# Four sums over the partitions: from products of ones on TensorE to GpSimd

## The chip, the cores and the metric

One core of a Trainium2 chip runs the whole program. The metric is the device time of one execution in microseconds (us); the number quoted for a kernel is the median of several runs. The engines are named as in the profile: PE (TensorE, matmuls), PEld (its weight loads), DVE (VectorE), ACT (ScalarE), POOL (GpSimd) and SP (SyncE, which issues most DMAs).

## The reference

Three transformer layers over 256 tokens of 1024 features, all in fp32: an attention layer with a squared-ReLU feed-forward of 4096 (the "first feed-forward"), then a layer with convolutions and a gated recurrence, then one with stick-breaking attention. The last two ("layer 0" and "layer 1" of the second block) are modulated by a vector `c`:

```
def ada_modulation(c, ada_w, ada_b):
    m = jax.nn.silu(c) @ ada_w + ada_b
    return jnp.split(m, N_MOD, axis=-1)
def modulate(h, shift, scale):
    return h * (1.0 + scale[:, None, :]) + shift[:, None, :]
```

`m` has 6 x 1024 columns: shift, scale and gate for the mixer, and the same for the feed-forward. Layer 0's `m` doesn't depend on the tokens, so it can be computed at any time before layer 0's first norm. Its first 2048 columns are the mixer's shift and scale (`SH_M`, `G_M`).

## The kernel before

**How `m` is made.** The 1024 rows of `ada_w` lie as 8 blocks of 128 partitions. DVE multiplies each block by the column of silu(c) that belongs to it and adds it to a tile `mod` of 128 x 6144 (`ada`, L1330, and `ada_mix`, L1342). What is left is the sum over the 128 partitions, which every partition needs. There are two ways to it in the kernel. `ada_sums` (L2226) is a product on PE with a 128x128 matrix of ones, 512 columns (CH) at a time into a PSUM bank (`sum_bank`), and `ada_parts` (L801) is ACT's copy of the bank back into `mod`. `partition_sums` (L656) is POOL's `partition_all_reduce` in SBUF, also by 512 columns. Sums 0 to 3 (`SH_M`, `G_M`) and 4 to 7 (the mixer's gate and the feed-forward's shift) go by PE, the others of layer 0 and all of layer 1 by POOL.

**Where sums 0 to 3 are.** The first 2048 columns of `mod` are complete when `mix_used` is 16, at the end of the first attention. PE computes sums 0 and 1 just ahead of the norm in front of the first feed-forward, sum 2 behind the transposes of token tile 0 and sum 3 ahead of those of tile 1, inside `entry(U_MLP, ...)`. `entry` is the norm with the first up unit in it: DVE writes the scaled xn, PE transposes it (L1882), ACT rounds it to `aT_hi` (L794), DVE takes the rest `aT_lo`, and PE multiplies (L1924).

**Weights in two parts.** Each weight part (128x1024, half a unit) is loaded to `w_raw` by SP, rounded by ACT to `w_hi` (`split_part`, L735), and DVE subtracts for the rest `w_lo` (`split_part`, L1158); PE multiplies with both. There are four slots. SP loads part v only behind `lo_done` of part v - 4; ACT rounds it only behind `w_used` of part v - 4, which PE counts up at each part that it is done with.

**The first feed-forward** runs 8 slices of 512 hidden features. From slice 1 on, slice j takes two up units into the banks ub and tp (L1910, L1912) and two down units of slice j - 1's hidden features (L1788 to L1791), eight parts in all. In each slice from 2 on DVE makes, in this order: an ada product (128x2048), w_lo of two parts, an addition from PSUM (`mlp_sum`, L1485), an ada product, w_lo of two parts, an addition from PSUM, w_lo of two parts, an ada product, w_lo of two parts, and the rest of the hidden features. The first four of these parts are the down units that PE takes in the same slice, the last four the up units of the next. ACT's relu (L934) waits for the second addition, and only behind relu and square does ACT round the next part. U_MLP is 16, so that `parts_to(U_MLP + 8)` is 48: `w_used` reaches it when PE is done with the up units of slice 2, and the up units of slices 3, 4 and 5 end at 56, 64 and 72.

**POOL** does small work for the norms (`half_var`), sits idle through the first feed-forward, and sums at 336 to 360 us and, four in a row each time, from 411, 484 and 594 us.

Of the kernel before, what the change touches and what calls it, by code (L numbers as in the profile page):

```python
# [39 lines left out]
UNIT = 2048  # L40
# [22 lines left out]
U_MLP = U_WO1 + 4  # L63
U_WIN = U_MLP + 4 * NJ_MLP
# [50 lines left out]
def block_program(nc, a, out):  # L115
    ctx = ExitStack()
    with ctx:
# [125 lines left out]

        def sum_bank(m):

            return (tp[:, 1, :] if m < 4 else acc[:, 1, :], ub[:, 0, :], ub[:, 1, :], acc[:, 2, :])[m % 4]

        def flat(h):
            return h.rearrange("p b n -> p (b n)")
# [363 lines left out]
        def _(pool):  # L613
# [72 lines left out]
            half_var(1, 0)  # L686
            half_var(0, 0)
            half_var(1, 0)
            half_var(0, 0)
            half_var(0, 0)  # L690
            half_var(1, 1)
# [21 lines left out]
        def _(act):  # L713
# [83 lines left out]
            def ada_parts(n0, n1):  # L797

                for n in range(n0, n1):
                    act.wait_ge(ada_sum, n + 1)  # L800
                    act.activation(mod[:, n * CH:(n + 1) * CH], sum_bank(n), ACT.Copy).then_inc(ada_out, 1)  # L801

            def copy_chunk(u, bank, ct):
# [77 lines left out]
            def mlp_norm(u):  # L881

                n_norm[0] += 1
                act.wait_ge(tile0_first, 1)
                half_square(0, 0, acc[:, 0, :], sq_half)
                act.wait_ge(tile0_done, 1)
                half_square(0, 1, acc[:, 1, :], sq_done)
                half_rstd(0, 1, 1)
                act.wait_ge(w_used, parts_to(u - 1))
                half_square(1, 0, acc[:, 2, :], sq_half)  # L890
                act.wait_ge(x_half, 1)
                half_square(0, 0, x[:, 0, 0:CH], sq_half)
                act.wait_ge(x_ready, 1)
                half_square(0, 1, x[:, 0, CH:D], sq_done)
                half_rstd(0, 1, 3)
                act.wait_ge(post_scaled, 2)
                half_square(1, 1, acc[:, 3, :], sq_done)
                half_rstd(1, 1, 2)
                norm_hi(1, 0)
                split_part(2 * u + 2)  # L900
                split_part(2 * u + 3)
                act.wait_ge(x_half, 2)
                half_square(1, 0, x[:, 1, 0:CH], sq_half)
                act.wait_ge(x_ready, 2)
                half_square(1, 1, x[:, 1, CH:D], sq_done)
                half_rstd(1, 1, 4)
                ada_parts(0, 2)
                norm_hi(1, 1)

            mlp_norm(U_MLP)  # L910

            def mlp_first(u):

                ada_parts(2, 4)
                split_hi(u + 2)
                act.wait_ge(w_used, parts_to(u + 2))
                act.activation(gtok, tp[:, :, :], ACT.Relu).then_inc(act_h, 1)
                split_hi(u + 3)
                act.wait_ge(h_T, 1)
                act.activation(hT_hi[:, :, :].rearrange("p (a b) n -> p a b n", a=2), blocks_in(acc[:, 0:2, :]),  # L920
                               ACT.Copy).then_inc(hT_hi_done, 1)
# [220 lines left out]
        def _(dve):  # L1142
# [386 lines left out]
            for j in range(NJ_MLP - 2, NJ_MLP):  # L1529
                mlp_slice(U_MLP + 4 * j - 2, j)  # L1530
            split_part(2 * U_WIN)
            ada_gain(0, 1, ada_out, 4)
            split_part(2 * U_WIN + 1)
            dve.wait_ge(gain_loaded[3], 16)
            dve.wait_ge(ada_gain_done, 1)
# [20 lines left out]
            for step, n in LRU_STEPS:  # L1556
                if step == "L":
                    split_lo(U_WIN + n)
                elif step == "E" and n == 0:
                    copy_chunk(U_WIN, acc[:, 1, :], T0["win"])  # L1560
                elif step == "T":
                    copy_T(uT, T0["win"], 4 * WIN_CHUNKS[n])
                elif step == "M" and n == 6:
                    ada(0, 5, 0, n, 22, dst=mod_next)
                elif step == "M":
                    ada(2, 4, 0, n, 23, src=ada_last, dst=mod_next)
                elif step == "I":
                    ada_gain(0, 4, pool_sum, 2)
                elif step == "P":
                    dve.wait_ge(lru_u, 2)  # L1570
                    dve.tensor_tensor(uT[:, 4:8, :], uT[:, 4:8, :], uT[:, 8:12, :], ALU.mult).then_inc(lru_p, 1)
                elif step == "D" and n == 0:
                    dve.wait_ge(lru_i, 1)
                    dve.wait_ge(lru_xr, 1)
                    dve.tensor_tensor(gate_i, gate_i, xr, ALU.mult).then_inc(lru_ix, 1)
                elif step == "C":
                    dve.wait_ge(cT_a, C0["win"] + 1)
                    dve.wait_ge(cT_v, C0["win"] + 1)
                    conv_last(xr, uT[:, 16:20, :], R_CONV_B, 4, R_CONV_BIAS)
                    conv_taps(xr, uT[:, 16:20, :], R_CONV_B, 4).then_inc(lru_xr, 1)  # L1580
                elif step == "K":
                    dve.wait_ge(lru_tap, 1)
                    conv_taps(conv_a, uT[:, 4:8, :], R_CONV_A, 3).then_inc(lru_conv, 1)
                elif step == "D" and n == 1:
                    dve.wait_ge(lru_a2, 1)
                    dve.wait_ge(lru_t, 1)
                    dve.scalar_tensor_tensor(lru_b, gate_r, 1.0, lru_b, ALU.add, ALU.mult).then_inc(lru_s2, 1)
                elif step == "Q":
                    dve.wait_ge(lru_sqrt, 1)
                    dve.wait_ge(lru_ix, 1)  # L1590
                    chained(dve.tensor_tensor(lru_b, lru_b, gate_i, ALU.mult))
                    for b in range(LB):
                        ins = dve.tensor_tensor_scan(lru_h[:, b, :], lru_a[:, b, :], lru_b[:, b, :], 0.0, ALU.mult, ALU.add)
                    chained(ins)
                elif step == "Y":
                    dve.wait_ge(lru_gelu, 1)
                    dve.tensor_tensor(lru_h, lru_h, uT[:, 12:16, :], ALU.mult).then_inc(lru_yb, 1)
                elif step == "R":
                    dve.wait_ge(lru_yb, 1)
                    dve.wait_ge(y_hi, 1)  # L1600
                    dve.tensor_tensor(hT_lo[:, :, :], lru_h, hT_hi[:, :, :].bitcast(F32),
                                      ALU.subtract).then_inc(y_lo, 1)
                elif step == "Z" and n == 0:
                    dve.wait_ge(lru_u, 3)
                    dve.wait_ge(lru_conv, 1)
                    dve.tensor_tensor(conv_a, conv_a, uT[:, 0:4, :], ALU.mult).then_inc(lru_ya, 1)
                elif step == "Z":
                    dve.wait_ge(y_hi, 2)
                    dve.tensor_tensor(aT_lo[:, 0:LB, :], conv_a, aT_hi[:, 0:LB, :].bitcast(F32),
                                      ALU.subtract).then_inc(y_lo, 1)  # L1610
# [3 lines left out]
            def swiglu(layer):  # L1614
# [49 lines left out]
                        for q in range(2):  # L1664
                            one(u + 5 + 3 * q + 12 * third, 2 + q + 4 * third, i, third if layer == 0 else None)
                if layer == 0:
                    ada_gain(1, 1, pool_sum, 8)
                one(u + 3 * NJ_SG - 4, NJ_SG - 1)

            swiglu(0)  # L1670
# [40 lines left out]
            for step, n in STICK_STEPS:  # L1711
                if step == "L":
                    split_part(2 * U_QKV2 + n)
                elif step == "R":
                    dve.wait_ge(qk_sq_done, n + 1)
                    dve.reduce_sum(qk_ss[:, :], qk_sq, AX.X).then_inc(qk_ss_done, 1)
                elif step == "E":
                    copy_v(U_QKV2 + 2 * n, n - 4)
                elif step == "N":
                    qk_norm(n)  # L1720
                elif step == "B":
                    copy_T(qkT, T0["qkv2"] + n, 4 * QKV_CHUNKS[n], qk_gain[:, n % 2:n % 2 + 1])
                elif step == "M":
                    stick_mask(n)
                elif step == "A":
                    stick_left_of(n)
                elif step == "D":
                    stick_weights(n)
                elif step == "K":
                    ada_gain(1, 4, pool_sum, 16)  # L1730
                elif step == "O":
                    dve.wait_ge(so_hi, n + 1)
                    bank, hi, lo = out_pairs(n)
                    bank_lo(lo, hi, bank).then_inc(so_lo, 1)
# [7 lines left out]
        def _(pe):  # L1742
# [484 lines left out]
                              stop=True).then_inc(ada_sum, 1)  # L2227

            pe.wait_ge(consts, 2)
            pe.wait_ge(mix_used, 16)  # L2230
            ada_sums(0, 2)
            entry(U_MLP, tp_banks, lambda: ada_sums(2, 3), lambda: ada_sums(3, 4), tile1_out=1)
            pe.wait_ge(ada_out, 4)

            def mlp_slice(j, i=None):
                u = U_MLP + 4 * j - 2
# [24 lines left out]
            pe.wait_ge(post_scaled, 3)  # L2261
            ada_sums(4, 6)

            entry(U_WIN, (acc[:, 0, :], acc[:, 1, :]), lambda: ada_sums(6, 7), lambda: ada_sums(7, 8), tile1_out=5)
            for step, n in LRU_STEPS:
                if step == "U" and 1 < n < 10:
                    c = n // 2
                    if n == 2:
                        pe.wait_ge(ada_out, 8)
                    if c == 2:  # L2270
                        pe.wait_ge(cT_a, C0["win"] + 1)
                        pe.wait_ge(cT_v, C0["win"] + 1)
# [150 lines left out]
```

## Time and profile before

| | us |
|---|---|
| median of 3 runs | 887.36 |
| lowest and highest | 887.23, 888.51 |
| the profiled execution | 887.93 |
| its span | 886.1 |
| PE busy | 875.6 (99%) |
| DVE busy | 711.1 (80%) |
| ACT busy | 492.2 (56%) |
| POOL busy | 94.1 (11%) |

The span is from the first instruction to the last of the profiled execution. Busy time of PE counts modelled ends of pipelined matmuls, so a busy PE isn't PE at its peak. A row in order of time reads: start, duration, engine, line, operation, output<-inputs, shapes, count, and in brackets the idle time of the engine just before it with what ended it. Neighbouring instructions of one kind are merged (x2, x4), and the duration is then that of all together.

### The profile page before, as it was taken

The numbers are of one execution on the slowest core, as the hardware profiler recorded it, in microseconds if no ns is written. First come the engines' busy times: TensorE is split into PE (matmuls) and PEld (weight loads), VectorE is DVE, ScalarE is ACT, GpSimd is POOL, SyncE is SP. The second block draws the span as 40 slices with busy tenths as digits, with TensorE's granted clock in tenths as the row PEclk, the third lists the DMA queues.
The fourth block names the chain that finished last, engine by engine and source line by source line (L and its number), as shares of the span: only waits on it lengthen the run. The fifth ranks groups of instructions, "written<-read, shape, count | busy, mean of one in ns | idle before, by whom it ended". The sixth has DMA issues, their size and how long they took to land.

```text
span 886.1 us, 13231 instructions
## 1 busy us (share of the span) xinstructions
PE 875.6 (99%) x4809; PEld 741.3 (84%) x4809; DVE 711.1 (80%) x730; ACT 492.2 (56%) x667; POOL 94.1 (11%) x74
## 2 busy tenths in 40 slices
PE   9999999999999999999999999999999999999998
PEld 5998878888888799879888888877777888888886
DVE  5698977988888987998998998689797865655655
ACT  6545665565556657755454455554676365545542
POOL 4000110000000104126101500034000100000000
PEclk9999999999999999999999999999999999999999
DMA  7989585899999484547999698545434376666661
GB/s 233 336 261 340 183 301 180 324 357 372 332 327 334 146 285 152 169 157 227 331 365 322 241 363 300 174 140 194 141 119 125 97 249 196 189 190 189 190 193 69
DMA packets 117096, 208.07 MB, mean 235 GB/s; under 512 B 7237, under 2 KB 81069, under 8 KB 111930
## 3 DMA queue, kind: packets, MB, share of 16 engines
q1 hardware_dynamic: 116566, 205.31, 68.3%
q10 hardware_dynamic: 292, 2.10, 0.7%
q8 instruction: 28, 0.46, 0.2%
q14 instruction: 18, 0.15, 0.0%
q0 software_dynamic: 192, 0.05, 0.0%
HBM read 206.39 MB, written 1.05 MB: 234 GB/s over the span
## 4 chain that ended last, share of the span: by engine, by line
PE 86%; DVE 8%; issue 2%; ACT 2%; DMA 1%; POOL 0%; DVEq 0%; SPq 0%; ACTq 0%; POOLq 0%
PE ub L1910 10%; PE tp L1910 10%; PE acc L1788 7%; PE acc L1789 7%; PE acc L1791 7%; PE ub L1912 5%; PE tp L1912 5%; PE acc L1751 5%; PE acc L1753 4%; PE acc L1752 4%; DVE w_lo L1158 3%; PE acc L1896 2%; PE acc L1898 2%; PE acc L1897 2%; PE tp L1973 2%
## 5 line engine op out<-in xcount | busy, mean ns | idle before, releaser
L1158 DVE TENSOR_TENSOR w_lo<-w_raw,w_hi 128x1024 fp32r<-128x1024 f32 x274 | 346.7, 1282 | 84.5 <-ACT w_hi L735 83.8
L735 ACT ACTIVATE w_hi<-w_raw 128x1024 fp32r<-128x1024 f32 x274 | 286.5, 1056 | 206.6 <-PE acc L1791 41.3
L1910 PE MATMUL tp<-aT,w_hi 128*128 128x512 f32 x432 | 135.9, 396 | 0.0
L1910 PE MATMUL ub<-aT,w_hi 128*128 128x512 f32 x432 | 135.4, 395 | 0.0
L1788 PE MATMUL acc<-w_hi,hT_hi 128*128 128x512 f32 x272 | 106.3, 391 | 1.1 <-DVE w_lo L1158 1.1
L1789 PE MATMUL acc<-w_lo,hT_hi 128*128 128x512 f32 x272 | 105.9, 389 | 0.0
L1791 PE MATMUL acc<-w_hi,hT_lo 128*128 128x512 f32 x264 | 102.7, 389 | 0.0
L1912 PEld LDWEIGHTS tp<-aT,w_lo 128*128 128x128 f32 x432 | 81.1, 188 | 19.2
L1912 PEld LDWEIGHTS ub<-aT,w_lo 128*128 128x128 f32 x432 | 81.1, 188 | 18.9
L1912 PE MATMUL tp<-aT,w_lo 128*128 128x256 f32 x432 | 84.9, 278 | 0.0
L1912 PE MATMUL ub<-aT,w_lo 128*128 128x256 f32 x432 | 84.9, 278 | 0.0
L1910 PEld LDWEIGHTS ub<-aT,w_hi 128*128 128x128 f32 x432 | 67.7, 189 | 1.9
L1910 PEld LDWEIGHTS tp<-aT,w_hi 128*128 128x128 f32 x432 | 65.8, 189 | 0.0
L1788 PEld LDWEIGHTS acc<-w_hi,hT_hi 128*128 128x128 f32 x272 | 51.0, 188 | 11.4 <-DVE w_lo L1158 1.2
L1330 DVE SCALAR_TENSOR_TENSOR mod<-ada_raw,silu_c,mod 128x2048 f32<-128x2048 f32 x24 | 58.3, 2431 | 1.2 <-DMA ada_raw<-in_l_ada_w 0.8
L1789 PEld LDWEIGHTS acc<-w_lo,hT_hi 128*128 128x128 f32 x272 | 51.1, 188 | 9.6
L1791 PEld LDWEIGHTS acc<-w_hi,hT_lo 128*128 128x128 f32 x264 | 49.6, 188 | 10.4
L1751 PE MATMUL acc<-w_hi,aT 128*128 128x512 f32 x140 | 56.7, 405 | 0.8 <-DVE scratch L1369 0.7
L1896 PE MATMUL acc<-aT,w_hi 128*128 128x256 f32 x192 | 55.3, 288 | 0.0
L1752 PE MATMUL acc<-w_lo,aT 128*128 128x512 f32 x140 | 54.7, 391 | 0.0
L1753 PE MATMUL acc<-w_hi,aT 128*128 128x512 f32 x140 | 54.6, 390 | 0.0
L1898 PE MATMUL acc<-aT,w_lo 128*128 128x256 f32 x192 | 54.3, 283 | 0.0
(321 smaller groups left out, 1399.4 us busy)
## 6 DMA issues: line engine op xcount, KB each, us to landing
ada_raw<-in_l_ada_w SPq DMA_DIRECT2D x24, 1024.0 KB, 7.2
w_raw<-in_l_ffn_w_gate SPq DMA_DIRECT2D x44, 512.0 KB, 4.6
w_raw<-in_l_ffn_w_up SPq DMA_DIRECT2D x44, 512.0 KB, 4.5
w_raw<-in_l_ffn_w_down SPq DMA_DIRECT2D x44, 512.0 KB, 4.1
w_raw<-in_w_up SPq DMA_DIRECT2D x32, 512.0 KB, 5.0
w_raw<-in_w_down SPq DMA_DIRECT2D x32, 512.0 KB, 5.6
scratch<-in_l_ada_w SPq DMA_DIRECT2D x14, 1024.0 KB, 7.8
w_raw<-in_attn_w_qkv SPq DMA_DIRECT2D x24, 512.0 KB, 6.9
```

The lines of the kernel that those rows point to most:

```text
L735: act.activation(rounded_part(v), w_raw[:, v % SLOTS, :], ACT.Copy).then_inc(hi_done, 1)
L1158: dve.tensor_tensor(rest_part(v), w_raw[:, v % SLOTS, :], rounded_part(v).bitcast(F32), ALU.subtract).then_inc(lo_done, 1)
L1751: pe.matmul(outp, op_hi[:, k + n, q], wh[:, c], start=start and n == 0, stop=False)
L1752: pe.matmul(outp, op_hi[:, k + n, q], wl[:, c], start=False, stop=False)
L1753: last = pe.matmul(outp, op_lo[:, k + n, q], wh[:, c], start=False, stop=stop and n == 1)
L1788: pe.matmul(outp, operand[0][:, k, q], wh[:, c], start=start, stop=False)
L1789: last = pe.matmul(outp, operand[0][:, k, q], wl[:, c], start=False, stop=False)
L1791: last = pe.matmul(outp, operand[1][:, k, q], wh[:, c], start=False, stop=stop)
L1896: pe.matmul(outp, wh, aT_hi[:, b, :], start=b == 0, stop=False)
L1898: last = pe.matmul(outp, wl, aT_hi[:, b, :], start=False, stop=b == KB - 1)
L1910: pe.matmul(banks[f], rounded_part(v)[:, c[f]], aT[:, :, b, :], start=b == 0, stop=False)
L1912: last = pe.matmul(banks[f][:, 0:TOK], rest_part(v)[:, c[f]], aT_hi[:, b, :], start=False, stop=b == KB - 1)
```

## The change

Sums 0 to 3 are taken from PE and ACT and given to POOL, between `half_var` calls in its order, one for each 8 parts of `w_used` from 48 on, in place in `mod`. PE's entry has no sums and no wait for `ada_out` any more, and the counts of `ada_out` and `pool_sum` move by four. The sums keep their 512 columns.

```diff
         def sum_bank(m):
-            return (tp[:, 1, :] if m < 4 else acc[:, 1, :], ub[:, 0, :], ub[:, 1, :], acc[:, 2, :])[m % 4]
+            return (acc[:, 1, :], ub[:, 0, :], ub[:, 1, :], acc[:, 2, :])[m % 4]
...
             half_var(1, 0)
+            pool.wait_ge(mix_used, 16)
+            partition_sums(mod[:, 0:UNIT], mod[:, 0:UNIT], w_used, parts_to(U_MLP + 8), 8)
             half_var(0, 0)
...
-                    act.wait_ge(ada_sum, n + 1)
+                    act.wait_ge(ada_sum, n - 3)
...
                 half_rstd(1, 1, 4)
-                ada_parts(0, 2)
                 norm_hi(1, 1)
...
             def mlp_first(u):
-                ada_parts(2, 4)
                 split_hi(u + 2)
...
-            ada_gain(0, 1, ada_out, 4)
+            ada_gain(0, 1, pool_sum, 4)
...
-                    ada_gain(0, 4, pool_sum, 2)
+                    ada_gain(0, 4, pool_sum, 6)
...
-                    ada_gain(1, 1, pool_sum, 8)
+                    ada_gain(1, 1, pool_sum, 12)
...
-                    ada_gain(1, 4, pool_sum, 16)
+                    ada_gain(1, 4, pool_sum, 20)
...
             pe.wait_ge(consts, 2)
-            pe.wait_ge(mix_used, 16)
-            ada_sums(0, 2)
-            entry(U_MLP, tp_banks, lambda: ada_sums(2, 3), lambda: ada_sums(3, 4), tile1_out=1)
-            pe.wait_ge(ada_out, 4)
+            entry(U_MLP, tp_banks, no_sums, no_sums)
...
-            entry(U_WIN, (acc[:, 0, :], acc[:, 1, :]), lambda: ada_sums(6, 7), lambda: ada_sums(7, 8), tile1_out=5)
+            entry(U_WIN, (acc[:, 0, :], acc[:, 1, :]), lambda: ada_sums(6, 7), lambda: ada_sums(7, 8), tile1_out=1)
...
-                        pe.wait_ge(ada_out, 8)
+                        pe.wait_ge(ada_out, 4)
```

## Rows read from the trace of the kernel before

**Rows 1.** Stretches: us; busy PE, PEld, DVE, ACT, POOL; clock, DMA share, GB/s
```profile
115.00:131.00 16.00, 15.99 (x70) 11.29 (x69) 11.10 (x16) 11.71 (x27) 0.84 (x3) 1.00 0.95 347
190.00:212.00 22.00, 22.00 (x114) 18.71 (x113) 20.05 (x16) 12.65 (x14) 0.00 (x0) 1.00 0.98 368
```

**Rows 2.** The chain of waits, 105 to 135 us: start, us, what
```profile
116.55 0.86 PE tp L2226 x2
...
119.56 0.86 PE ub L2226 x2
...
124.08 0.86 PE acc L2226 x2
...
126.11 7.27 PE tp L1924 x32
```

**Rows 3.** Weight loads (PEld) in order of time at the norm
```profile
118.25 0.42 PEld L1882 LDWEIGHTS acc<-ident,xn 128*128 128x128 f32 x4 [0.81 <-DVE xn L1181]
...
119.83 0.19 PEld L1924 LDWEIGHTS tp<-w_hi,aT 128*128 128x128 f32 x1 [0.24 <-ACT aT L794]
...
124.79 0.42 PEld L1882 LDWEIGHTS acc<-ident,xn 128*128 128x128 f32 x4 [0.68 <-DVE xn L1181]
125.45 0.42 PEld L1882 LDWEIGHTS acc<-ident,xn 128*128 128x128 f32 x4 [0.24 <-DVE xn L1181]
```

**Rows 4.** Weight loads (PEld) of the down units, slices 2 to 5
```profile
168.44 0.19 PEld L1788 LDWEIGHTS acc<-w_hi,hT_hi 128*128 128x128 f32 x1 [0.68 <-DVE w_lo L1158]
...
173.79 0.19 PEld L1788 LDWEIGHTS acc<-w_hi,hT_hi 128*128 128x128 f32 x1
...
195.82 0.19 PEld L1788 LDWEIGHTS acc<-w_hi,hT_hi 128*128 128x128 f32 x1
...
217.85 0.19 PEld L1788 LDWEIGHTS acc<-w_hi,hT_hi 128*128 128x128 f32 x1
...
239.88 0.19 PEld L1788 LDWEIGHTS acc<-w_hi,hT_hi 128*128 128x128 f32 x1
```

**Rows 5.** ACT in order of time, slices 2, 3 and at 343 us
```profile
168.00 1.06 ACT L735 ACTIVATE w_hi<-w_raw 128x1024 fp32r<-128x1024 f32 x1 [0.57 <-PE tp L1912]
...
175.29 1.06 ACT L934 ACTIVATE scratch<-scratch 128x1024 f32<-128x1024 f32 x1 [1.64 <-DVE scratch L1485]
...
190.79 1.07 ACT L735 ACTIVATE w_hi<-w_raw 128x1024 fp32r<-128x1024 f32 x1 [0.57 <-PE tp L1912]
...
343.24 1.06 ACT L735 ACTIVATE w_hi<-w_raw 128x1024 fp32r<-128x1024 f32 x1 [1.82 <-PE acc L1898]
```

**Rows 6.** POOL in order of time
```profile
335.91 4.25 POOL L656 PARTITION_ALL_REDUCE mod<-mod  x1 [28.77 <-PE acc L1898]
343.25 3.23 POOL L656 PARTITION_ALL_REDUCE mod<-mod  x1 [3.09 <-PE acc L1898]
...
411.03 13.68 POOL L656 PARTITION_ALL_REDUCE mod<-ada_raw  x4 [8.18 <-issue]
```

**Rows 7.** Line L1158 from 131 to 290 us, durations in ns
```profile
L1158 DVE TENSOR_TENSOR w_lo<-w_raw,w_hi x57: 1215/1220/1226, 131.4 to 282.8; 128x1024 fp32r<-128x1024 f32 x57
```

**Rows 8.** DVE in order of time, beside POOL's sums
```profile
336.97 3.27 DVE L1158 TENSOR_TENSOR w_lo<-w_raw,w_hi 128x1024 fp32r<-128x1024 f32 x1
...
415.02 0.68 DVE L1642 TENSOR_TENSOR scratch<-scratch,ub 128x512 f32<-128x512 f32 x1
```

**Rows 9.** DVE in order of time, slices 2 to 5
```profile
172.30 2.36 DVE L1158 TENSOR_TENSOR w_lo<-w_raw,w_hi 128x1024 fp32r<-128x1024 f32 x2
...
192.63 1.22 DVE L1158 TENSOR_TENSOR w_lo<-w_raw,w_hi 128x1024 fp32r<-128x1024 f32 x1
...
212.96 1.22 DVE L1158 TENSOR_TENSOR w_lo<-w_raw,w_hi 128x1024 fp32r<-128x1024 f32 x1
...
234.47 1.22 DVE L1158 TENSOR_TENSOR w_lo<-w_raw,w_hi 128x1024 fp32r<-128x1024 f32 x1
```

**Rows 10.** DVE's groups of instructions, 216 to 238 us
```profile
L1158 DVE TENSOR_TENSOR w_lo<-w_raw,w_hi 128x1024 fp32r<-128x1024 f32 x8 | 9.7, 1222 | 3.3 <-ACT w_hi L735 3.3
```

## The prediction

> **What bounds the kernel now.** I read the stretches first (busy time of each engine, granted clock, DMA share), since the change removes work at one place and adds it at another. At the norm before the first feed-forward (115 to 131 us) PE is booked as busy for 15.99 of 16.00 us, in a slice of the feed-forward for 22.00 of 22.00, both at a granted clock of 1.00; there DVE is busy 20.05 of 22.00 us [rows 1]. So PE looks like the bound at both places, and DVE is close behind it in the feed-forward, which is what a second view has to qualify.
>
> The chain of waits at the norm books 0.86 us for each sum of ones: sums 0 and 1 run from 116.55 into the transposes (the row shown is the first of two alike), sum 2 at 119.56, sum 3 at 124.08 [rows 2]. Four of them are 3.44 us that the change takes from PE, and the chain counts them as on the path. The weight loads of the same stretch (PEld) say something else: the transposes at 118.25, 124.79 and 125.45 each wait for DVE's xn, 0.81, 0.68 and 0.24 us, and the first product behind the transposes of tile 0 waits 0.24 us for ACT's aT at 119.83 [rows 3]. Where PEld sits idle right behind a sum and is released by another engine, the sum filled a wait.
>
> In the feed-forward the weight loads show when each half unit ("part") is first used, and DVE's rows when its rest w_lo is ready. In slice 2 PE waits 0.68 us for DVE at 168.44 already [rows 4].
>
> **Part 1, the norm.** Four products of ones leave PE, four copies leave ACT, and two waits on ada_out leave PE.
> - Sums 0 and 1 sit ahead of the transposes of tile 0, which start when DVE's xn is there [rows 3]. Gain 0.
> - Sum 2 sits between those transposes and the first product. Without it that product could start at 119.83 instead of 120.42 (119.56 + 0.86), 0.59 us sooner [rows 2, 3]. It isn't kept: the next thing that PE does behind these products is sum 3 and the transposes of tile 1, and these wait for DVE at 124.79. DVE's xn hangs on rstd, which hangs on ACT's squares of x, none of which waits for a product of this stretch. Gain 0.
> - Sum 3 ends at 124.94 (124.08 + 0.86); the transposes can go at 124.79 [rows 2, 3]. Gain at most 0.15, and the second four wait for xn until 125.45 either way. I take 0.05.
> - ACT's copies lie where it waits for PE or DVE next, so they give nothing.
> So the norm gives 0.05 us, with 0 below and 3.44 above (the whole of the four sums) as the far bound. What it gives must also get past slice 2, where PE waits for DVE.
>
> **Part 2, the feed-forward.** POOL now does four partition_all_reduce of 128x512 (mod is four of CH columns), one each when w_used reaches 48, 56, 64 and 72. w_used 48 is the end of the second up unit of slice 2, and the others come one slice later each. ACT's split in slice 2 at 168.00 waits for the same value, and 190.79 is the one of slice 3 [rows 5]. That POOL starts as promptly shows later on: ACT's split at 343.24 and POOL's sum at 343.25 are released together [rows 5, 6].
>
> Nobody waits for the results (ada_gain asks much later). What costs is DVE. w_lo takes 1.22 us in all 57 rows of the feed-forward, where POOL now does nothing [rows 7]. Beside the sum of 335.91 one takes 3.27: 2.05 more. Beside the four sums from 411.03 an addition from PSUM takes its usual 0.68 [rows 6, 8]. So each sum holds back the next DVE instruction with two SBUF inputs by 2.05 us, once, from the end of the one in flight. The Trainium skill (GPSIMD Engine Reference, Key points) says that GpSimd shares its SBUF interfaces with VectorE, with contention for instructions with two SBUF inputs; the 3.27 beside the 0.68 agrees, and by it each of the four sums costs DVE time wherever w_lo or an ada product runs.
>
> Now where DVE stands against PE. Third part of each slice's four down parts, w_lo ready and first use [rows 4, 9]:
> - slice 2: ready at 172.30 + 1.22 = 173.52, used at 173.79, 0.27 ahead
> - slice 3: 192.63 + 1.22 = 193.85, used at 195.82, 1.97 ahead
> - slice 4: 212.96 + 1.22 = 214.18, used at 217.85, 3.67 ahead
> - slice 5: 234.47 + 1.22 = 235.69, used at 239.88, 4.19 ahead
>
> The sum of slice 2 starts at 168.00, when the w_lo that releases PE at 168.44 [rows 4] is in flight; the w_lo behind it is then stalled by 2.05, all of DVE's queue behind that is 2.05 later, and PE waits 2.05 - 0.27 = 1.78 us. If the stall falls one instruction later, the PSUM addition behind hides 0.60 of it and PE waits 1.18.
>
> Does DVE get its time back before the next sum? Its idle gap at the end of slice 2 waits for a w_hi that ACT can make only behind its relu, and that relu waits 1.64 us for DVE's own addition (175.29) [rows 5]: the gap moves along with DVE. So I let DVE's lateness stand through slices 3 and 4. From slice 4 on DVE has 3.3 us of gaps a slice [rows 10]; I count 1.1 of them as recovered (the gap before the last part of the slice and the wait of ACT that isn't behind relu), a choice between 0 and 3.3. The lateness of DVE, and PE's as far as it exceeds the lead:
> - slice 2: 2.05, PE +1.78
> - slice 3: 4.10, less 1.97: PE +2.13 in all
> - slice 4: 6.15, less 3.67: PE +2.48 in all
> - slice 5: 6.15 - 1.1 + 2.05 = 7.10, less 4.19: PE +2.91 in all
> Behind slice 5 no sum is left, and DVE catches up under PE's remaining slices. Bounds: if every gap absorbs, only slice 2 counts, 1.2 to 1.8; with nothing recovered the last line is 8.20 - 4.19 = 4.0.
>
> **Part 3, the rest.** ada_out 4 for 8 and 1 for 5, pool_sum's counts and the bank of sums 0 to 3 change numbers only. POOL's rstd work at the next norm comes two slices behind the last sum. 0 both.
>
> **Sum.** 2.91 - 0.05 = +2.86 us. The profiled execution took 887.93 us (span 886.1 and 1.8 around it), 0.57 above the median of 887.36; it would become 890.8, and the median 890.2. A measurement of this kernel can tell 0.2% (1.8 us) from no change.
>
> **The rivals.**
> - *Hidden stalls.* DVE's gaps take up the lateness, or the stalls fall on PSUM additions: +0 to +1.7. For: DVE has 9 to 15% of a slice idle [rows 1, 10]. Against: the lead of 0.27 in slice 2. About 888.4. Chance 0.22.
> - *The norm gives back more (the other side).* If the chain of waits is right and PE, not xn, sets the entry, the four sums are worth up to 3.44 at 116 to 125 us. It decides the sign once the entry comes out earlier by more than the feed-forward loses; with the least loss of 1.2 that is 887.36 - 3.44 + 1.2 = 885.1. Against: PEld's waits for xn right behind the sums. Chance 0.08.
> - *The stalls feed on themselves.* w_raw of part v + 4 is loaded only behind w_lo of part v, with DMA 0.98 busy [rows 1]. If late loads add one more stall of 2.05 in slices 4 and 5 with nothing recovered: 4.0 + 1 to 2: 892.5 to 893.5. Chance 0.07.
> - *The clock.* The sums keep PE going while it waits at the norm. Without them it stands still some 1.7 us at 116.5 (two times 0.86) and 1.1 at 123.7. The granted clock is 1.00 there now [rows 1]. The products that follow take 7.27 us in one row to the end of the entry [rows 2]; at 1.2 instead of 2.4 GHz they would take that much more: 890.2 + 7.3 = 897.5. The Trainium skill (TensorE: Matmul & The Clock Gate, Why this matters for your kernels) ties a fall to idle time of PE. No row here has it fall; chance 0.02.
> The forecast, PE held by DVE in slices 2 to 5 for 1.8 to 4.0 us, has 0.61.
>
> **How the numbers follow.** Faster by over 0.2%: only the second rival, 0.08. Slower: the forecast, nearly whole, the third and the fourth, 0.68. Same: 0.24. The range leaves out the second rival and the last one: 887.0 (hidden stalls and a little of the norm) to 892.4. The likeliest case's own is 889.1 to 891.4.
>
> **What would show it.** Right: DVE's w_lo or ada product with one instance 2.05 us longer than its like right behind POOL's sums at about 168, 192, 215 and 237; PE waiting near 2 us for w_lo in slice 2 and some tenths in slices 3 to 5; the transposes of tile 1 still starting at about 124.8, now with over 1 us of idle PEld before them. Wrong: no wait of PE for w_lo beyond 0.7 in slice 2; or the entry's last product much before 133; or a stall shorter than 2.05.

## The result: 1.8 to 2.0 us slower, nearly all of it in slice 2

| | before | after |
|---|---|---|
| median, 22 runs of each | 887.62 | 889.64 |
| the profiled execution | 887.93 | 890.53 |
| its span | 886.1 | 888.7 |

The ratio is 1.0020, 95% interval 1.0014 to 1.0027, so +1.8 us with 1.2 to 2.4 around it; the medians stand 2.02 us apart. One run of the kernel before took 957.08 us, a slow one, and counts in its median but not in the ratio. Forecast were 890.2 us and +2.86.

**Where the time went, by PE's weight loads.** The places are those of each kernel's profiled execution. I measure three stretches by their first loads, so that the start of the execution doesn't matter: "norm" from the first transpose of xn to the first load into ub of slice 1, "1 to 3" from there to the first load into ub of slice 3, "1 to 7" to the first load of slice 7's down units.

| | norm | 1 to 3 | 1 to 7 |
|---|---|---|---|
| before | 14.75 | 46.24 | 145.60 |
| after | 14.70 | 47.97 | 147.33 |
| difference | -0.05 | +1.73 | +1.73 |

PE gains 0.05 us at the norm, loses 1.73 us in slice 2 and nothing in slices 3 to 6.

POOL in order of time, the kernel after (start, us, what; in brackets the idle time before it):

```profile
167.89 3.30 POOL L656 PARTITION_ALL_REDUCE mod<-mod  x1 [45.22 <-PE tp L1912]
192.29 7.52 POOL L656 PARTITION_ALL_REDUCE mod<-mod  x1 [21.10 <-PE tp L1912]
214.30 5.82 POOL L656 PARTITION_ALL_REDUCE mod<-mod  x1 [14.50 <-PE tp L1912]
236.33 3.88 POOL L656 PARTITION_ALL_REDUCE mod<-mod  x1 [16.20 <-PE tp L1912]
```

The four sums start where they were forecast. Their lengths are not the same: 3.30, 7.52, 5.82 and 3.88 us. DVE in order of time, the kernel after, slices 2 to 5:

```profile
167.99 3.26 DVE L1158 TENSOR_TENSOR w_lo<-w_raw,w_hi 128x1024 fp32r<-128x1024 f32 x1
171.18 0.67 DVE L1485 TENSOR_TENSOR scratch<-scratch,ub 128x512 f32<-128x512 f32 x1
171.78 2.34 DVE L1330 SCALAR_TENSOR_TENSOR mod<-ada_raw,silu_c,mod 128x2048 f32<-128x2048 f32 x1
174.04 2.35 DVE L1158 TENSOR_TENSOR w_lo<-w_raw,w_hi 128x1024 fp32r<-128x1024 f32 x2
...
194.36 2.35 DVE L1158 TENSOR_TENSOR w_lo<-w_raw,w_hi 128x1024 fp32r<-128x1024 f32 x2
196.63 0.68 DVE L1485 TENSOR_TENSOR scratch<-scratch,tp 128x512 f32<-128x512 f32 x1
197.25 2.65 DVE L1158 TENSOR_TENSOR w_lo<-w_raw,w_hi 128x1024 fp32r<-128x1024 f32 x1
200.47 1.23 DVE L1158 TENSOR_TENSOR w_lo<-w_raw,w_hi 128x1024 fp32r<-128x1024 f32 x1 [0.58 <-ACT w_hi L737]
...
218.07 2.15 DVE L1158 TENSOR_TENSOR w_lo<-w_raw,w_hi 128x1024 fp32r<-128x1024 f32 x1 [0.44 <-ACT w_hi L737]
...
237.37 2.93 DVE L1158 TENSOR_TENSOR w_lo<-w_raw,w_hi 128x1024 fp32r<-128x1024 f32 x1 [0.25 <-ACT w_hi L737]
```

Each sum holds back one w_lo, whose usual 1.22 us [rows 7] become 3.26, 2.65, 2.15 and 2.93. Line the ends up (start and duration added): the sums end at 171.19, 199.81, 220.12 and 240.21, the held w_lo at 171.25, 199.90, 220.22 and 240.30. So POOL holds DVE in the last stretch of a sum. A sum that gets in at once lasts 3.3 us, a longer one has waited to get in. The addition from PSUM at 171.18 takes its 0.67. Note where the held w_lo stands: in slices 3 and 4 behind the slice's second addition (the one from tp), in slice 5 ahead of it; that addition is at 240.22 there.

PE's weight loads, the kernel after, slice 2; answers to [rows 4]:

```profile
168.13 0.19 PEld L1788 LDWEIGHTS acc<-w_hi,hT_hi 128*128 128x128 f32 x1 [0.67 <-DVE w_lo L1158]
...
171.31 0.19 PEld L1788 LDWEIGHTS acc<-w_hi,hT_hi 128*128 128x128 f32 x1 [0.59 <-DVE w_lo L1158]
...
175.30 0.19 PEld L1788 LDWEIGHTS acc<-w_hi,hT_hi 128*128 128x128 f32 x1 [1.40 <-DVE w_lo L1158]
```

The wait at 168.13 is the 0.68 of before. The other two are new: 0.59 for the held w_lo itself and 1.40 for the third part, late with DVE's whole queue. In slices 3 to 5 PE's loads of the down units wait for nobody.

The norm, the kernel after, weight loads; answers to [rows 3]:

```profile
117.99 0.42 PEld L1882 LDWEIGHTS acc<-ident,xn 128*128 128x128 f32 x4 [2.18 <-issue]
118.59 0.42 PEld L1882 LDWEIGHTS acc<-ident,xn 128*128 128x128 f32 x4 [0.18 <-DVE xn L1181]
119.34 1.35 PEld L1924 LDWEIGHTS tp<-w_hi,aT 128*128 128x128 f32 x4 [0.33 <-ACT aT L796]
...
124.47 0.47 PEld L1882 LDWEIGHTS acc<-ident,xn 128*128 128x128 f32 x4 [0.16 <-DVE xn L1181]
```

From the first transposes to those of tile 1 it takes 6.48 us (117.99 to 124.47), before 6.54 (118.25 to 124.79 [rows 3]): xn sets it with the sums and without. But where the forecast saw over 1 us of idle PEld ahead of 124.8, the row at 124.47 has 0.16. What filled the rest stands in the stretches of the kernel after (us; busy PE, PEld, DVE, ACT, POOL; clock, DMA share, GB/s):

```profile
115.00:118.00 3.00, 1.23 (x6) 0.70 (x5) 2.84 (x6) 2.83 (x9) 0.32 (x2) 1.00 1.00 415
118.00:119.00 1.00, 0.98 (x8) 0.82 (x8) 1.00 (x2) 0.52 (x3) 0.00 (x0) 1.00 0.99 418
119.00:120.00 1.00, 0.91 (x5) 0.58 (x4) 1.00 (x3) 1.00 (x3) 0.00 (x0) 0.58 1.01 426
120.00:122.00 2.00, 2.00 (x6) 1.58 (x5) 2.00 (x3) 2.00 (x3) 0.00 (x0) 0.50 1.03 434
122.00:123.00 1.00, 1.00 (x5) 0.76 (x4) 0.19 (x1) 1.00 (x4) 0.21 (x1) 0.72 0.92 345
```

PE, busy for 1.23 of the 3.00 us up to 118, ran at the lower of its two levels (0.50 is 1.2 GHz) from about 119.2 to 122.6. Its first 16 products took longer for it, but ended before xn of tile 1 was there. The Trainium skill (TensorE: Matmul & The Clock Gate, Why this matters for your kernels) ties a fall to idle time of PE; the fall behind this idle stretch agrees, and the experiments show that it doesn't come each time. In a second execution of the same kernel (e9 below) the clock stayed at 1.00, and there PEld sits idle ahead of tile 1 as forecast:

```profile
123.95 0.42 PEld L1882 LDWEIGHTS acc<-ident,xn 128*128 128x128 f32 x4 [1.35 <-DVE xn L1181]
```

**The rest of the profiled 2.60 us.** The kernel after reaches the norm 0.26 us sooner (117.99, before 118.25), and the norm and slice 2 make 1.68; that leaves 1.18. It lies behind POOL's four sums of layer 1: from their start to the end of the span it takes 292.4 us in the kernel before (593.76 to 886.1) and 293.6 in the kernel after (595.15 to 888.7). As they begin, the kernel after has a w_lo of 3.15 us:

```profile
595.32 3.15 DVE L1158 TENSOR_TENSOR w_lo<-w_raw,w_hi 128x1024 fp32r<-128x1024 f32 x1 [1.37 <-ACT w_hi L737]
```

In the kernel before, the w_lo in flight there took 1.23 (593.43). In the traces of all eleven experiments that last stretch takes 292.3 to 292.5 us. The second execution of the same kernel (e9) has 1.23 there again and a span of 887.1, 1.7 above one of the kernel before (e10, 885.4). So the 1.2 belong to that one execution and not to the change.

### The profile page after: what moved, and what is told of

Same layout as the page of the kernel before. It is cut to its first block, busy times and chain, and to the rows that moved or that the text cites. A ratio compares the mean times of both kernels' runs of the same rounds, so it can differ in the third digit from the quotient of the medians.

```text
span 888.7 us, 13218 instructions
## 1 busy us (share of the span) xinstructions
PE 874.7 (98%) x4801; PEld 740.5 (83%) x4801; DVE 717.2 (81%) x730; ACT 489.8 (55%) x663; POOL 113.8 (13%) x78
## 4 chain that ended last, share of the span: by engine, by line
PE 83%; DVE 9%; issue 3%; ACT 2%; DMA 1%; POOL 0%; DVEq 0%; SPq 0%; ACTq 0%; POOLq 0%
PE ub L1910 10%; PE tp L1910 10%; PE acc L1788 7%; PE acc L1789 7%; PE acc L1791 6%; PE ub L1912 5%; PE tp L1912 5%; PE acc L1751 4%; PE acc L1752 4%; PE acc L1753 4%; DVE w_lo L1158 4%; PE acc L1896 2%; PE acc L1898 2%; PE acc L1897 2%; PE tp L1973 2%
## 5 line engine op out<-in xcount | busy, mean ns | idle before, releaser
L1158 DVE TENSOR_TENSOR w_lo<-w_raw,w_hi 128x1024 fp32r<-128x1024 f32 x274 | 352.8, 1305 | 80.9 <-ACT w_hi L737 80.7
L656 POOL PARTITION_ALL_REDUCE mod<-mod x14 | 56.7, 4087 | 197.2 <-PE tp L1912 97.0
```

The source lines that it names most:

```text
L1158: dve.tensor_tensor(rest_part(v), w_raw[:, v % SLOTS, :], rounded_part(v).bitcast(F32), ALU.subtract).then_inc(lo_done, 1)
```

## The experiments

Two theories stood against each other. A: a sum holds back one DVE instruction with two SBUF inputs, and this costs only where DVE's lead over PE (how long before PE's first use a w_lo is ready) is short, so all in slice 2. B: the loss sits elsewhere, in the norm without the sums (clock, entry) or in other places of the program. All diffs but that of e3 are against the kernel after; "held" is what a DVE instruction took above its usual time. The kernel before on the same chip stands behind each median. Kernels e1 to e4 shared one chip, e5 to e8 one, e9 to e11 one.

**e1: the four sums one slice later** (190, 212, 234, 256 us in place of 168 to 236).

```diff
-            partition_sums(mod[:, 0:UNIT], mod[:, 0:UNIT], w_used, parts_to(U_MLP + 8), 8)
+            partition_sums(mod[:, 0:UNIT], mod[:, 0:UNIT], w_used, parts_to(U_MLP + 12), 8)
```

> The changed kernel with its four sums one slice later (w_used 56, 64, 72, 80). Theory A: the loss is the one stall of 2.05 us in slice 2, where DVE is only 0.27 us ahead of PE. Then no PE wait for w_lo over 0.7 us in slices 2 to 6, and the time is that of the kernel before within 0.4 us, some 1.8 us below the changed one. Rival B: the loss comes from the norm (PE idle there, and its clock at half for 3 us); then it stays at +1.8 us over the kernel before. Rival C: lateness adds up from sum to sum, as in the prediction; then slices 3 to 6 still cost 0.5 to 1 us.

Measured: 887.42 (887.61), ratio 1.0002 (0.9993 to 1.0011); norm 14.68, 1 to 3 46.28, 1 to 7 145.64. The loss is gone with the four sums still there. DVE in order of time, e1, slice 3:

```profile
193.88 0.68 DVE L1485 TENSOR_TENSOR scratch<-scratch,tp 128x512 f32<-128x512 f32 x1
194.47 2.67 DVE L1158 TENSOR_TENSOR w_lo<-w_raw,w_hi 128x1024 fp32r<-128x1024 f32 x1
197.72 1.23 DVE L1158 TENSOR_TENSOR w_lo<-w_raw,w_hi 128x1024 fp32r<-128x1024 f32 x1 [0.58 <-ACT w_hi L737]
```

The held w_lo (1.45 too long) comes right behind the second addition. The next w_lo waits for ACT's w_hi either way: here by 0.58 us, in the kernel before by 1.95:

```profile
198.75 1.22 DVE L1158 TENSOR_TENSOR w_lo<-w_raw,w_hi 128x1024 fp32r<-128x1024 f32 x1 [1.95 <-ACT w_hi L735]
```

The gap takes the stall. The third and fourth sums of e1 hold a w_lo ahead of the second addition (2.93 at 234.96, and of two merged 4.40 at 255.86), and PE loses nothing by them either (1 to 7 145.64): in slice 5 DVE's lead is 4.19 us [rows 4, 9], more than a stall.

**e2: no sums in the feed-forward at all**; `SH_M` and `G_M` are left without their sum over the partitions.

```diff
-            pool.wait_ge(mix_used, 16)
-            partition_sums(mod[:, 0:UNIT], mod[:, 0:UNIT], w_used, parts_to(U_MLP + 8), 8)
...
-            ada_gain(0, 1, pool_sum, 4)
+            ada_gain(0, 1, mix_used, 16)
```

> The changed kernel without the four sums of the feed-forward (sums 0 to 3 over the partitions are left out, so shift and scale of layer 0's mixer are unsummed). It shows the norm's part alone: no products of ones, PE idle. Theory A: 0 to -0.1 us against the kernel before, although the granted clock falls to half near 120 us. Rival B: +1.5 to +2 us. The far bound of the prediction, 3.4 us gained, would show as 884.2.

Measured: 887.84 (887.61), 1.0005 (0.9996 to 1.0014); norm 14.85, 1 to 3 46.28. Half of the change, PE's, is worth nothing that can be seen: the interval leaves out a gain of over 0.4 us, so 3.44 and 0.6 too, and in the trace the norm is 0.10 longer, not 0.15 shorter. The clock was at 0.5 from 118.94 in this execution.

**e3: both, the products of ones on PE and four spare sums on POOL**, against the kernel before.

```diff
+            for n in range(4):
+                pool.wait_ge(w_used, parts_to(U_MLP + 8) + 8 * n)
...
+                part = gate_ffn[:, n % 2 * CH:(n % 2 + 1) * CH]
+                pool.partition_all_reduce(part, part, P, bass.bass_isa.ReduceOp.add).then_inc(spare_sum, 1)
```

> The kernel before, with its products of ones kept, plus four sums on POOL that nothing uses, of 128x512 in place in gate_ffn, at the same four counts of w_used. Theory A: +1.8 us over the kernel before, a w_lo of 3.27 us near 168 us and PE waiting about 2 us in all in slice 2. Rival B: within 0.3 us of the kernel before.

Measured: 889.14 (887.61), 1.0018 (1.0009 to 1.0028); norm 14.74, 1 to 3 47.97. The whole loss, with nothing taken from PE and the clock at 1.00. POOL in order of time, e3, gives the pattern of the kernel after to within 0.1 us (3.30, 7.52, 5.83 and 3.88), and PE waits nearly the same, 0.55 (0.59) and 1.40:

```profile
171.37 0.19 PEld L1797 LDWEIGHTS acc<-w_hi,hT_hi 128*128 128x128 f32 x1 [0.55 <-DVE w_lo L1167]
...
175.37 0.19 PEld L1797 LDWEIGHTS acc<-w_hi,hT_hi 128*128 128x128 f32 x1 [1.40 <-DVE w_lo L1167]
```
 So the price is that of the sums' place and not of what they sum.

**e4: one part later** (w_used 49, 57, 65, 73), where DVE is in its ada product.

```diff
-            partition_sums(mod[:, 0:UNIT], mod[:, 0:UNIT], w_used, parts_to(U_MLP + 8), 8)
+            partition_sums(mod[:, 0:UNIT], mod[:, 0:UNIT], w_used, parts_to(U_MLP + 8) + 1, 8)
```

> The changed kernel with each sum one part later (w_used 49, 57, 65, 73), so that in slice 2 it starts near 171 us, with an ada product in flight on DVE, and two w_lo behind it that PE needs. If POOL gets in at the end of whatever is in flight: the w_lo behind the ada product takes 3.27, PE waits about 1.8 us and the time is that of the changed kernel. If POOL is passed over behind an ada product until DVE's next addition from PSUM or gap (as the trace of the changed kernel suggests, where the sum of 192.29 lasts 7.52 us): its span is over 5 us, the w_lo behind the PSUM addition is the longer one, PE doesn't wait, and the time is that of the kernel before within 0.4 us.

Measured: 888.90 (887.61), 1.0013 (1.0004 to 1.0022); 1 to 3 47.97. POOL got in at the end of the ada product, the first w_lo behind it was held by 2.05, and PE lost the same 1.73, now in one wait. My idea that a sum asked for during an ada product is always passed over fell. The weight loads of e4:

```profile
168.35 0.19 PEld L1788 LDWEIGHTS acc<-w_hi,hT_hi 128*128 128x128 f32 x1 [0.65 <-DVE w_lo L1158]
...
175.52 0.19 PEld L1788 LDWEIGHTS acc<-w_hi,hT_hi 128*128 128x128 f32 x1 [1.86 <-DVE w_lo L1158]
```

**e5: four parts later** (52, 60, 68, 76), in the second half of each slice, where I took DVE's lead to be ample. The diff is that of e4 with `+ 4`.

> The changed kernel with each sum four parts later (w_used 52, 60, 68, 76): in slice 2 it starts near 179 us, when DVE is 1.9 us or more ahead of PE for every part that follows. Theory A (a sum costs PE 2.05 us less the lead of the w_lo that it holds back): 0 to 0.3 us over the kernel before. If it were the slice and not the lead that counts: +1.8 us as in the changed kernel.

Measured: 889.53 (887.10), 1.0027 (1.0015 to 1.0038); 1 to 3 46.27, 1 to 7 147.01. A clear miss: it costs as much as the change. DVE in order of time, e5 (of two w_lo merged, usually 2.35):

```profile
180.79 4.40 DVE L1158 TENSOR_TENSOR w_lo<-w_raw,w_hi 128x1024 fp32r<-128x1024 f32 x2
...
203.16 4.40 DVE L1158 TENSOR_TENSOR w_lo<-w_raw,w_hi 128x1024 fp32r<-128x1024 f32 x2
...
225.53 4.40 DVE L1158 TENSOR_TENSOR w_lo<-w_raw,w_hi 128x1024 fp32r<-128x1024 f32 x2
...
247.90 4.40 DVE L1158 TENSOR_TENSOR w_lo<-w_raw,w_hi 128x1024 fp32r<-128x1024 f32 x2
```

Each of the four sums holds a w_lo by the full 2.05, ahead of both additions of the next slice. PE falls back a little in every slice (0.32 by the end of slice 3's up units, then 0.66, 1.01, 1.41). The size can be worked out: without a sum DVE comes round in 20.33 us (192.63 to 212.96 [rows 9]) and PE in 22.03 (195.82 to 217.85 [rows 4]), so DVE gains 1.70 a slice. A full stall of 2.05 in each slice is 0.35 more than that. The rows above lie 22.37 apart, 0.34 over PE's 22.03: DVE sets the pace. Here lateness does add up from slice to slice, as the prediction had it for the change. Behind slice 7's start PE waits for DVE twice more (0.40 at 290.11, 0.65 at 294.71), and POOL's sum of 335.05 us in e10 is at 337.08 here, so the whole is some 2.0 us.

**e6: one part earlier** (47, 55, 63, 71), so that the stall falls on the w_lo that PE already waits for. The diff is that of e4 with `- 1`.

> The changed kernel with each sum one part earlier (w_used 47, 55, 63, 71): in slice 2 it starts near 165 us beside an ada product, and the w_lo behind it is one that PE waits for already, so its lead is 0. Theory A: that w_lo takes 3.27 us, PE loses the whole 2.05 us there and nothing more in slices 3 to 5; 2.05 us over the kernel before, 0.3 more than the changed one. If the loss is limited to what the changed kernel shows whatever the lead: +1.7 us.

Measured: 890.58 (887.10), 1.0042 (1.0030 to 1.0053); 1 to 3 48.28: 2.04 lost where 2.05 was expected. PE's weight loads of e6 have one wait in place of three:

```profile
169.31 0.19 PEld L1788 LDWEIGHTS acc<-w_hi,hT_hi 128*128 128x128 f32 x1 [2.70 <-DVE w_lo L1158]
```

0.65 of it were there before. With a lead of nothing a sum costs its whole 2.05. The other three sums held ada products by 1.4 (3.73 for 2.34), and PE lost nothing by them. The median is 1.4 above what the trace accounts for, and the profiled execution (888.76) is the lowest of the seven runs. The clock recorded for each run sorts them: the three at 0.999 or more have a median of 889.08, which is what the trace accounts for (887.10 + 2.04), and the four at 0.996 to 0.998 took 890.58 to 892.45. No trace of one of those four exists, so where the time went in them isn't shown.

**e7: two sums at once in slice 2**, the other two in slices 3 and 4.

```diff
+            partition_sums(mod[:, 0:CH], mod[:, 0:CH], w_used, parts_to(U_MLP + 8), 8)
+            partition_sums(mod[:, CH:UNIT], mod[:, CH:UNIT], w_used, parts_to(U_MLP + 8), 8)
```

> The changed kernel with two of the four sums in slice 2, back to back (w_used 48, 48, 56, 64). Theory A: the second holds back one more instruction of DVE ahead of the w_lo that has 0.27 us of lead, so PE loses 2 x 2.05 - 0.27 = 3.8 us. If the second is passed over until an addition from PSUM, the w_lo behind has a lead of nearly 3 us and the loss stays at 1.8.

Measured: 892.45 (887.10), 1.0060 (1.0043 to 1.0077); norm 15.15, 1 to 3 49.43. DVE in order of time, e7 (the first row is two w_lo, of which the second is held):

```profile
166.87 4.40 DVE L1159 TENSOR_TENSOR w_lo<-w_raw,w_hi 128x1024 fp32r<-128x1024 f32 x2
171.19 0.67 DVE L1486 TENSOR_TENSOR scratch<-scratch,ub 128x512 f32<-128x512 f32 x1
171.79 3.80 DVE L1331 SCALAR_TENSOR_TENSOR mod<-ada_raw,silu_c,mod 128x2048 f32<-128x2048 f32 x1
```

The second sum starts during the PSUM addition, which goes on undisturbed and hides 0.6 of it; the ada product behind is held by 1.45. PE lost 3.19 in slice 2 (3.8 expected, less that 0.6). This is the prediction's own remark, that an addition hides 0.60, seen at work. The median is 1.8 above what the trace accounts for (887.10 + 3.19 + 0.40); the profiled execution (890.82, clock 0.998) is again the lowest, and the other three, all at 0.996, took 892.44 to 892.69. The norm's extra 0.40 is the clock:

```profile
118.00:119.00 1.00, 1.00 (x7) 0.81 (x5) 1.00 (x3) 0.60 (x1) 0.00 (x0) 0.60 1.06 451
119.00:120.00 1.00, 1.00 (x5) 0.81 (x4) 1.00 (x3) 0.72 (x2) 0.00 (x0) 0.50 1.01 426
120.00:122.00 2.00, 2.00 (x7) 1.57 (x6) 1.76 (x3) 2.00 (x3) 0.00 (x0) 0.60 0.98 413
```

**e8: all four sums in one go in slice 5**, where the lead was 4.19.

```diff
+            partition_sums(mod[:, 0:UNIT], mod[:, 0:UNIT], w_used, parts_to(U_MLP + 20), 0)
```

> The changed kernel with all four sums back to back from the middle of slice 5 (w_used 72), where DVE leads by 4.0 to 5.9 us and has 3.3 us of gaps a slice. If lateness adds up as the prediction had it, 8.2 us of stalls less at most 3 of gaps against a lead of 4.0 to 4.2: PE loses 1 to 2.5 us. If the stalls fall mostly before gaps, as those of slices 3 to 5 did in the changed kernel: under 0.3 us.

Measured: 888.57 (887.10), 1.0015 (1.0005 to 1.0024); 1 to 3 46.24, 1 to 7 145.69, then some 1.0 lost by the transposes of the next norm (302.45). Four DVE instructions were held, by 1.8, 1.5, 1.5 and 2.0: 6.8 us in all, of which the lead of 4.19 and the gaps took all but 1.0.

**e9 and e10: the kernel after and the kernel before once more**, one execution each.

> The changed kernel once more, for a second trace. Its first trace loses 1.73 us in slice 2 and another 1.19 us near 600 us, where a w_lo that POOL's sum just missed in the kernel before is held back. Theory A: only the loss in slice 2 belongs to the change, and the second is a matter of which came first in that execution: slice 2 again 1.7 us, near 600 us nothing or 1.2. If the second belongs to the change it is there again, and a span near 888.7 with it.

> The kernel before once more, for a second trace. No loss in slice 2; if the loss near 600 us can befall it too, its span is 886.1 or 887.3.

Measured: 888.88 and 887.17 (886.97). In e9 slices 1 to 3 lose 1.73 again (1 to 3 47.97, 1 to 7 147.32), the clock stays at 1.00 and the norm takes 14.72. In e10 they are 46.25, 145.60 and 14.75.

**e11: sums one slice later, and PE kept going at the norm** by four products of ones whose results nobody reads, against e1.

```diff
+            def spare_products(n0, n1):
+                for n in range(n0, n1):
+                    pe.matmul(ub[:, n % 2, :], ones[:, :], mod[:, n * CH:(n + 1) * CH], start=True, stop=True)
...
+            spare_products(0, 2)
+            entry(U_MLP, tp_banks, lambda: spare_products(2, 3), lambda: spare_products(3, 4))
```

> The changed kernel with its four sums one slice later and with PE kept busy at the norm by the four products of ones, whose results nothing reads. It shows what the idle of PE and the fall of the clock at the norm cost. Theory A (both lie in the wait for DVE's xn): the granted clock stays at 1.00, and the entry's end and the time are those of the variant with the sums one slice later, within 0.4 us of the kernel before. If idle PE costs by the clock: 0.2 to 0.5 us faster than the variants without products.

Measured: 887.41 (886.97), 1.0008 (0.9998 to 1.0018); norm 14.75, 1 to 7 145.60. The same as e1 and as the kernel before. The four products cost nothing and give nothing: neither direction of the change's first half can be measured.

## Why the prediction was right, and by how much it was off

- **The norm: right, in place and size.** Forecast 0.05, measured 0.05 (14.75 to 14.70 in the kernel after, 14.68 in e1). e2 and e11 show the chain of waits' 3.44 us of sums to be worth nothing: PE filled its wait for xn with them.
- **The stall of one sum: right in kind, and in size for slice 2.** One DVE instruction with two SBUF inputs is held, by 2.05 at most (3.26 for 1.22), and additions from PSUM are not. The other three stalls were 1.43, 0.93 and 1.71 us, and a stall shorter than 2.05 was one of the prediction's own signs of being wrong. e3 shows that the sums alone cause the loss, e1 that without their place in slice 2 there is none.
- **Slice 2: right.** 2.05 less the lead of 0.27 was to cost 1.78; it cost 1.73. The lead works as a subtraction: with no lead 2.04 (e6), with two sums 3.19 (e7).
- **"Behind the first sum lateness adds up": the term that was mis-sized.** The forecast put 1.13 us (2.91 - 1.78) on slices 3 to 5; they cost 0.00. One half of the step held: DVE is still 2.04 late against the start of slice 1 when it reaches the third part of slice 3 (194.36, before 192.63 [rows 9], with slice 1 0.31 earlier), so the gap did move along. The other half didn't. I let each sum stall DVE from the end of the instruction in flight, ahead of the second addition. In slices 3 and 4 POOL got in only about when that addition ran, and held the w_lo behind it. ACT's relu and the next w_hi hang on the addition, not on this w_lo. So the stalls, 1.43 and 0.93 us, ran beside ACT's work and ended in gaps that were there anyway (1.95 before, 0.58 after; 1.76 before at 219.63, 0.84 after at 221.06). In slice 5 the stall of 1.71 did fall ahead of the second addition. By then DVE had caught up (its third part is at 235.90, before 234.47, which is no later than PE is), its lead of 4.19 took the stall, and no sum came behind it. e5 is the other case: full stalls ahead of the additions in four slices running, and it does add up. The bound "if every gap absorbs, only slice 2 counts, 1.2 to 1.8" was the one that came true.
- **The sum.** 1.73 - 0.05 = 1.68 from the trace, against 2.86 forecast and 1.8 (1.2 to 2.4) by the ratio. The median of 889.64 lies near the forecast 890.2 partly by luck: the forecast has 1.13 us for slices 3 to 5 that weren't there, the measured medians stand 0.3 further apart than the traces account for, and the kernel before itself measured 0.26 higher than the 887.36 that the forecast started from.
- **The rivals.** Hidden stalls: true for slices 3 to 5, not for slice 2. Its "up to 1.7" and the forecast's "1.8 to 4.0" meet where the measured time lies, so the time alone doesn't tell them apart; the waits of 0.59 and 1.40 in slice 2 speak for the forecast, the missing "some tenths in slices 3 to 5" for the rival. More given back by the norm: refuted by e2. Stalls that feed on themselves through late loads: no extra held instruction in slices 4 and 5.
- **The clock: likelier than its chance of 0.02, and far cheaper than its price of 7.3 us.** Without the products of ones it fell to 0.50 at 118 to 120 us in four of nine profiled executions (the kernel after, e2, e4, e7) and stayed in five (e1, e5, e6, e8, e9); with work on PE there it stayed in all four (before, e3, e10, e11). The stretch at 1.2 GHz lasted some 3 us and not to the end of the entry, and most of it lay in PE's wait for xn: it cost 0 in the kernel after and in e4, 0.10 to 0.15 in e2, 0.40 to 0.45 in e7. The loss is there without any fall: 1.53 us between the medians in e3, 1.7 between the spans of e9 and e10. But the clock recorded for each run says that falls are common. It is 0.997 or 0.998 in the four profiled executions with the fall and at least 0.999 in the others. Of the kernels without the products 46 of 84 runs have 0.998 or less (14 of 22 of the kernel after); of those with work on PE there none of 85. In the kernel after the median of these 14 is 889.71, of the other eight 888.61; in e1 887.85 and 887.09. How much of that the fall makes isn't shown: two executions of the kernel before, neither with a fall, reach the norm 0.9 us apart (118.25, and 117.35 in e10). So some tenths of the medians' 1.8 to 2.0 may be the clock's.

**Still open.** Why POOL gets in at once when it is asked for during some DVE instructions (the w_lo at 168, the ada product in e4, that in e5 at 178.5) and only 4 us later during others (slice 3, in e1 too), with DVE's queue as dense in both. Those later ones got in as an addition from PSUM began: counted back 3.2 us from their ends, at 196.6 and 216.9 in the kernel after (additions at 196.63 and 216.95) and at 193.9 and 214.2 in e1 (193.88 and 214.20). What lets the others in sooner no run here tells. Nor did any version beat the kernel before: e1 and e11, the best places found for the sums, are equal to it.

## What to carry to other kernels

Taking work from the busiest engine pays only where that engine isn't waiting for another at that place; look at the waits of its weight loads right behind the work, not at its share of busy time or at the chain. A partition sum on an idle GpSimd isn't free: price it as one stall of VectorE, subtract VectorE's lead over its consumer at that very instruction, and ask which instruction's end opens the next gap. Here a stall behind that instruction ran into the gap and was free; one ahead of it used up lead, which cost nothing while the lead lasted (slice 5, e1) and added up where a stall came in every slice (e5).

## What the runs showed of the hardware that I had not expected

- A partition_all_reduce of 128x512 takes 3.2 us once it gets in, but a span of 3.3 to 7.5 us in the profile, by what DVE does as it is asked for. The held DVE instruction ends 0.06 to 0.10 us behind it.
- The Trainium skill (GPSIMD Engine Reference, Key points) names contention for instructions with two SBUF inputs; the runs agree (3.26 for 1.22 with w_lo, 3.80 for 2.35 with the ada product, 0.67 as ever with an input from PSUM).
- PE's clock fell in some executions of a kernel and not in others (the kernel after and e9 are the same kernel), behind the same stretch of little work: 1.23 us busy of 3.00 in the kernel after, which fell, 1.21 of 3.00 in e1, which didn't.
